# The down projection of a decoder layer as seven block products over sliding ranges of k pairs

## The reference

```python
def _conv_ffn(xn, s_ffn, p):
    u = xn @ p['ffn_w_in']                          # 2048 -> 2 * 5632
    u, buf = _causal_dwconv(u, s_ffn, ...)
    a, b = jnp.split(u, 2, axis=-1)
    return (jax.nn.silu(a) * b) @ p['ffn_w_out'], buf   # 5632 -> 2048
...
    f, f_new = _conv_ffn(xn, s_ffn, p)
    x = x + _rmsnorm(f, p['n_ffn_post'])
```

## Time and profile before

| | |
|---|---|
| time, median of 3 runs | 2547.48 us (2547.18 to 2551.67) |
| time of the profiled execution | 2549.71 us |
| its span, first to last instruction | 2547.8 us |
| PE busy | 2497.7 us, 98% |
| DVE busy | 1620.7 us, 64% |
| ACT busy | 921.5 us, 36% |
| POOL busy | 392.0 us, 15% |
| moved by transfers | 303.32 MB |

### The profile page before, as it was taken

The page is one execution under the profiler, slowest core; times in us unless marked ns, Lnnn a source line. Parts: engine busy times, 40 slices in busy tenths (PEclk is TensorE's granted clock), DMA queues, the critical chain, the costliest instruction groups (busy, mean ns, idle before and its releaser), DMA issues. The chain is left out here.

```text
span 2547.8 us, 48784 instructions
## 1 busy us (share of the span) xinstructions
PE 2497.7 (98%) x20582; PEld 2467.6 (97%) x20582; DVE 1620.7 (64%) x2395; ACT 921.5 (36%) x1324; POOL 392.0 (15%) x208
## 2 busy tenths in 40 slices
PE   7999999999999999999999999999999999999997
PEld 7999999999999999999999999999999999999996
DVE  6544545766146368898889888888998333333226
ACT  5332222433214235444444444444445212122112
POOL 3333222433233352000000000000000000000005
PEclk9999999999999999999999999999999999999998
DMA  4222237622373424233333333333335423232422
GB/s 174 90 82 93 76 111 263 216 76 73 108 257 111 157 67 143 93 98 112 108 114 109 106 106 110 109 106 114 114 106 170 150 75 130 91 122 95 157 84 88
DMA packets 97415, 303.32 MB, mean 119 GB/s; under 512 B 10160, under 2 KB 14896, under 8 KB 96320
## 3 DMA queue, kind: packets, MB, share of 16 engines
q1 hardware_dynamic: 58336, 211.84, 26.3%
q10 hardware_dynamic: 38880, 88.59, 9.6%
HBM read 255.77 MB, written 44.62 MB: 118 GB/s over the span
## 5 line engine op out<-in xcount | busy, mean ns | idle before, releaser
L1313 PE MATMUL psum_proj<-x_hi,w_hi 128*128 128x288 f32 (+2 forms) x1696 | 511.0, 301 | 15.7 <-DVE x_lo L1959 13.6
L1313 PE MATMUL psum_proj<-x_lo,w_hi 128*128 128x288 f32 (+2 forms) x1696 | 501.3, 296 | 0.0
L1315 PE MATMUL psum_proj<-x_hi,w_lo 128*128 128x288 f32 (+2 forms) x1696 | 500.9, 295 | 0.0
L525 POOL TENSOR_TENSOR w_lo<-raw,w_hi 128x1024 fp32r<-128x1024 f32 x128 | 322.0, 2518 | 620.1 <-ACT w_hi L611 620.1
L1313 PEld LDWEIGHTS psum_proj<-x_hi,w_hi 128*128 128x128 f32 x1696 | 320.9, 189 | 23.0 <-issue 16.2
L1313 PEld LDWEIGHTS psum_proj<-x_lo,w_hi 128*128 128x128 f32 x1696 | 320.1, 189 | 2.7 <-issue 1.9
L611 ACT ACTIVATE w_hi<-raw 128x1024 fp32r<-128x1024 f32 x138 | 145.2, 1056 | 487.8 <-PE psum_proj L1315 412.3
L1315 PEld LDWEIGHTS psum_proj<-x_hi,w_lo 128*128 128x128 f32 x1696 | 319.9, 189 | 0.0
L1814 PE MATMUL psum_proj<-ops_a,w_hi 128*128 128x288 f32 x890 | 262.3, 295 | 1.1 <-DVE w_lo L2676 0.7
L1816 PE MATMUL psum_proj<-ops_a,w_lo 128*128 128x288 f32 x890 | 262.1, 295 | 0.0
L1815 PE MATMUL psum_proj<-ops_a,w_hi 128*128 128x288 f32 x890 | 261.9, 294 | 0.0
(11 more groups left out here) (428 smaller groups left out, 6255.5 us busy)
## 6 DMA issues: line engine op xcount, KB each, us to landing
raw<-in_weights_dram SPq DMA_DIRECT2D x386, 512.0 KB, 3.6
g_spill<-x_flat ACTq DMA_DIRECT2D x44, 288.0 KB, 2.1
spill<-tail ACTq DMA_DIRECT2D x24, 288.0 KB, 2.1
arena<-in_xT_dram SPq DMA_DIRECT2D x4, 1152.0 KB, 11.3
y_spill<-arena ACTq DMA_DIRECT2D x4, 1152.0 KB, 5.1
h_spill<-arena ACTq DMA_DIRECT2D x8, 576.0 KB, 2.9
x_hi<-h_spill ACTq DMA_DIRECT2D x1, 4608.0 KB, 19.0
x_flat<-g_spill ACTq DMA_DIRECT2D x5, 864.0 KB, 9.0
```

The source lines that it names most:

```text
L525: nc.gpsimd.tensor_tensor(w_lo[:, slot], raw[:, r], w_hi[:, slot].bitcast(F32), ALU.subtract).then_inc(lo_ready, 1)
L1313: nc.tensor.matmul(banks[:, n, 0:b - a], w_hi[:, slot, k], (hi, lo)[part][:, a:b], start=first and part == 0, stop=False)
L1315: mm = nc.tensor.matmul(banks[:, n, 0:b - a], w_lo[:, slot, k], hi[:, a:b], start=False, stop=last)
```

## The change

The down projection is done as the up projection is: seven block products for two output tiles by two k tiles (a k pair, `kp`). The first 42 k tiles make 21 pairs (`DOWN_KP`), the 16 output tiles make 8 pairs j. A step is one (j, kp), 7 * 3 = 21 matmuls; two steps are a unit, and the 84 down units go on in the same loops, rings and routines as the 160 up units (`ALL_UNITS`). The last two k tiles stay as `last_down`.

The seven products are linear in k, so they are summed over k before they are combined. `WINDOWS` cuts the 21 pairs for each j into five ranges of 2 to 5 pairs, shifted against each other from j to j, so that 40 passes (`PASSES`) are run, 8 for each range r. A pass leaves seven products in seven banks, and the next starts one bank further on. `take_pass` on ACT copies them out: in range 0 into the arena, where each j has seven accumulators (`m_of`), later into a staging buffer `m_stage`. From there GpSimd adds them to the accumulators with two accumulating transfers per pass, of four and of three products (590 and 442 thousand bytes), 60 transfers in all for the 30 passes `STAGED`. ACT waits for the previous one (`m_acc`) before it writes its half of `m_stage` again. The last two passes (`BY_VE`) are added by DVE. `combine` on DVE turns the seven accumulators into the output pair.

The gate rows of a pair are read by SP (`kp_load`, 590 thousand bytes), in the same queue as the weights, into one of five slots. DVE makes three sums (`g_first`, `g_second`, `g_third`), ACT the high parts of all seven operands (`g_highs`, 2016 columns) and DVE the low parts (`g_lows`, 2016). `freed` gives the unit after which a slot is free and `g_made_at` the unit at which a pair is made. The input rows of the residual, 16 by 576, come back in two transfers (`h_load`, 10 rows and 6) in SP's queue instead of one in ACT's. The matmuls of the down projection fall from 4224 to 168 * 21 + 192 = 3720.

```diff
+DOWN_KP, DOWN_PAIRS = FT // 2 - 1, KT // 2
+WINDOWS = ((2, 5, 5, 5, 4),) * 4 + ((3, 5, 5, 5, 3),) * 2 + ((4, 5, 5, 4, 3), (5, 5, 5, 3, 3))
+PASSES = [(r, j, sum(WINDOWS[j][:r]), sum(WINDOWS[j][:r + 1])) for r in range(5) for j in range(DOWN_PAIRS)]
+STEPS = [(p, kp) for p, (r, j, first, stop) in enumerate(PASSES) for kp in range(first, stop)]
+FIRST_STEP = [sum(q < p for q, kp in STEPS) for p in range(len(PASSES))]
+END_STEP = [sum(q <= p for q, kp in STEPS) - 1 for p in range(len(PASSES))]
...
+G_SLOTS = 5
...
+BY_VE = (len(PASSES) - 2, len(PASSES) - 1)
+STAGED = [p for p, (r, j, first, stop) in enumerate(PASSES) if r and p not in BY_VE]
...
+DOWN_PRODUCTS = ((A11, G11), (A12, G21), (S2, G2), (S3, G3), (S1, G1), (S4, G22), (A22, G4))
+M_AT = (0, 2, 3, 1, 5, 6, 4)
+M_SPLIT = 4
...
+        def freed(kp):
+            if kp < 4:
+                return WUNITS - 4 + kp // 2
+            if kp == 4:
+                return WUNITS + 2
+            return WUNITS + LAST_USE[kp - G_SLOTS] // 2
+        g_made_at = {WUNITS - 2: 0, WUNITS - 1: 1, WUNITS + 2: 2, WUNITS + 5: 3, WUNITS + 7: 4}
+        for _kp in range(5, DOWN_KP):
+            g_made_at[max(freed(_kp) + 2, max(g_made_at) + 1)] = _kp
...
+            def kp_load(kp):
+                if kp == 4:
+                    sp.wait_ge(taken, DOWN_TAKEN0)
...
+                    sp.wait_ge(g_st, 16 * FT)
+                else:
+                    sp.wait_ge(units_done, W_UNIT0 + freed(kp) + 1)
+                    sp.wait_ge(g_st, 16 * (2 * kp + 2))
+                sp.dma_start(g_sums(kp)[:, 0:1152].rearrange("p (n t) -> p n t", n=2),
+                             g_spill[2 * kp:2 * kp + 2].rearrange("n p t -> p n t")).then_inc(block_in[kp % G_SLOTS], 16)
...
+            for w in range(2, ALL_UNITS + 2):
+                unit = W_UNIT0 + w
                 sp.wait_ge(lo_ready, unit - 1)
-                sp.wait_ge(ws_ready, unit - 1 - W_UNIT0)
+                sp.wait_ge(ws_ready, w - 1)
                 sp.dma_start(raw[:, unit % 2], weights[unit]).then_inc(raw_in[unit % 2], 16)
-            weights_in((DOWN_UNIT0 + 2) // 2, UNITS // 2)
+                for kp in range(DOWN_KP):
+                    if freed(kp) + 3 == w:
+                        kp_load(kp)
...
+                if w == H_FREED + 3:
+                    sp.wait_ge(units_done, W_UNIT0 + H_FREED + 1)
+                    h_load(0, H_FIRST)
...
+            for p in STAGED:
+                j = PASSES[p][1]
+                for half, (first, stop) in enumerate(((0, M_SPLIT), (M_SPLIT, 7))):
+                    pool.wait_ge(*product_out(p, stop - 1))
+                    pool.dma_start(m_of(j, first, stop), m_stage[:, first * HALF:stop * HALF], accum_op=ALU.add)\
+                        .then_inc(m_acc[half], 16)
...
+            def g_highs(kp):
+                act.wait_ge(op_sum, KP + kp + 1)
+                nc.scalar.activation(g_high_part(kp), g_sums(kp), ACT.Copy).then_inc(op_high, 1)
...
+            def take_pass(p):
+                r, j, first, stop = PASSES[p]
+                for q in range(7):
+                    act.wait_ge(*product_done(p, q))
+                    if r == 0:
+                        to = m_of(j, M_AT[q], M_AT[q] + 1)
+                    else:
+                        to = m_stage[:, M_AT[q] * HALF:(M_AT[q] + 1) * HALF]
+                        before = STAGED.index(p)
+                        if before and q in (0, M_SPLIT):
+                            act.wait_ge(m_acc[q // M_SPLIT], 16 * before)
+                    nc.scalar.activation(to, bank(7 * p + q), ACT.Copy).then_inc(part_out, 1)
...
+            for w in range(3, ALL_UNITS):
                 g, u = STD + w // UP_UNITS, w % UP_UNITS
-                more = w + 2 < WUNITS
+                more = w + 2 < ALL_UNITS
+                conv = STD < g <= FT
+                step = 2 * (w - WUNITS)
                 if more:
                     hi_a(w + 2)
...
-                if w == WUNITS - 3:
...
+                if u == 3 and w < WUNITS:
                     p1_copy(g)
+                if step in END_STEP and END_STEP.index(step) not in BY_VE:
+                    take_pass(END_STEP.index(step))
                 if more:
                     hi_s(w + 2)
...
-                if w == WUNITS - 2:
...
-                if w == WUNITS - 2:
...
+                if step + 1 in END_STEP and END_STEP.index(step + 1) not in BY_VE:
+                    take_pass(END_STEP.index(step + 1))
+                if w in g_made_at:
+                    g_highs(g_made_at[w])
...
+            def down_step(s):
+                p, kp = STEPS[s]
+                w, kk = WUNITS + s // 2, s % 2
+                hi, lo = w_slot(w, 0), w_slot(w, 1)
+                first, last = s == FIRST_STEP[p], s == END_STEP[p]
+                if kk == 0:
+                    pe.wait_ge(lo_ready, W_UNIT0 + w + 1)
+                    pe.wait_ge(wl_ready, w + 1)
+                pe.wait_ge(op_low, G_OPS0 + kp + 1)
+                for q, (wp, go) in enumerate(DOWN_PRODUCTS):
+                    if first:
+                        if q == 0:
+                            pe.wait_ge(*(product_out(p - 2, 6) if p >= 2 else (taken, up_taken(FT - 1) + 6 * p)))
+                        elif p >= 1:
+                            pe.wait_ge(*product_out(p - 1, q - 1))
+                        else:
+                            pe.wait_ge(*((part_out, FT - STD) if q == 1 else (taken, up_taken(FT - 1) + q - 1)))
+                    mm = three(bank(7 * p + q), hi[:, 2 * wp + kk], lo[:, 2 * wp + kk], cut(g_high_part(kp), go),
+                               cut(g_low_part(kp), go), first, last)
+                    if last and (q < 6 or kk == 0):
+                        mm.then_inc(tile_mm, 1)
+                if kk:
+                    mm.then_inc(units_done, 1)
...
+            def g_first(kp):
+                f = g_sums(kp).rearrange("p (n t) -> p n t", n=7)
+                ve.wait_ge(*kp_landed(kp % G_SLOTS, kp // G_SLOTS + 1))
+                own(tt_op(f[:, G3:G1 + 1], f[:, G4:G4 + 1].broadcast_to([P, 2, HALF]), f[:, G22:G11 + 1], ALU.subtract))
+                return steps[0]
+            def g_second(kp, first_step):
+                f = g_views(kp)
+                ve.wait_ge(own_step, first_step)
+                own(tt_op(f[G2], f[G1], f[G22], ALU.subtract))
+                return steps[0]
+            def g_third(kp, second_step):
+                f = g_views(kp)
+                ve.wait_ge(own_step, second_step)
+                tt_op(f[G4], f[G21], f[G2], ALU.add).then_inc(op_sum, 1)
+            def g_lows(kp):
+                ve.wait_ge(op_high, G_OPS0 + kp + 1)
+                ve.wait_ge(op_sum, KP + kp + 1)
+                tt_op(g_low_part(kp), g_sums(kp), g_high_part(kp).bitcast(F32), ALU.subtract).then_inc(op_low, 1)
...
+            def take_pass(p):
+                j = PASSES[p][1]
+                for half in range(2):
+                    ve.wait_ge(m_acc[half], accumulated(p))
+                for q in range(7):
+                    ve.wait_ge(*product_done(p, q))
+                    m = m_of(j, M_AT[q], M_AT[q] + 1)
+                    tt_op(m, bank(7 * p + q), m, ALU.add).then_inc(taken, 1)
...
+            for w in range(3, ALL_UNITS):
                 g, u = STD + w // UP_UNITS, w % UP_UNITS
-                if w + 1 < WUNITS:
+                conv, kp = STD < g <= FT, g_made_at.get(w)
+                step = 2 * (w - WUNITS)
+                if w + 1 < ALL_UNITS:
                     direct_lows(w + 1)
-                if w + 2 < WUNITS:
+                if w + 2 < ALL_UNITS:
                     first_step = sums_first(w + 2)
-                if w + 1 < WUNITS:
+                if step in END_STEP and END_STEP.index(step) in BY_VE:
+                    take_pass(END_STEP.index(step))
+                if w + 1 < ALL_UNITS:
                     sum_lows(w + 1)
-                if w + 2 < WUNITS:
+                if kp is not None:
+                    g_first_step = g_first(kp)
+                if w + 2 < ALL_UNITS:
                     second_step = sums_second(w + 2, first_step)
-                if g > STD and u < 2:
+                if kp is not None:
+                    g_second_step = g_second(kp, g_first_step)
+                if conv and u < 2:
                     tap_one(g - 1, u)
-                if w + 2 < WUNITS:
+                if w + 2 < ALL_UNITS:
                     sums_third(w + 2, second_step)
-                if g > STD and u < 2:
+                if kp is not None:
+                    g_third(kp, g_second_step)
+                if conv and u < 2:
                     tap_two(g - 1, u)
...
-                if w == WUNITS - 2:
...
+                if u == 3 and w < WUNITS:
                     evacuate(g)
-            taps_of(FT - 1, 0)
...
+                if w in combined_at:
+                    combine(combined_at[w])
+                if kp is not None:
+                    g_lows(kp)
...
```

(23 more changed lines are left out.)

365 lines of the change are left out of this document (155 added, 210 removed).

## The result

| | before | after |
|---|---|---|
| time, median of 4 runs each | 2549.16 us | 2567.99 us (2566.59 to 2570.01) |
| span of the profiled execution | 2547.8 us | 2564.9 us |
| matmuls and other TensorE instructions | 20582 | 20078 |

The ratio is 1.0074, with a 95% interval from 1.0057 to 1.0091: the changed kernel is slower, although it does 504 matmuls less. The forecast was 2557 us, 11 less than measured.

The account below looks back on a forecast made before the run. TensorE, busy 2497.7 of 2547.8 us, was taken to bound the kernel. 2549.7 - 66.7 (matmuls) - 0.7 (old waits) + 74.3 (new waits) + 2 (clock) = 2558.6 us profiled; the median, 2.2 lower, 2557 us; range 2510 to 2605.

Parts of the forecast that it names:

- the case that the prediction gave as its forecast: Whole kernel: new TensorE waits of 68 to 85 us, time 2550 to 2567 us; chance 0.38.
- rival 2: Down projection: accumulations fill the transfer engines, weights come late, ScalarE waits for m_acc; 2585 to 2620 us; 0.17 with all above 2567.
- The gain: Down projection on TensorE: 504 fewer matmuls at 0.1323 us each save 66.7 us, also the break-even for new waits.
- What makes the waits: Down projection: preparing a pair takes 5.5 us or more of VectorE's queue against 2.2 us room, delaying the next weights.
- Rival 1: Down projection: VectorE, 77% busy, hides nearly all; up to 35 us of waits, 2480 to 2515 us; 0.22 for below 2534.
- waits for L1225: Sign in the down stage: TensorE would have few waits for ScalarE's copies if the forecast was right.
- The waits by stretch: Last up group to tail tiles: queues moved forward give 74.3 us at factor 2, 17.8 of it in units 63 to 83.
- The accumulations: Accumulating transfers cost twice their bytes in engine time, 5.3 us per interval; waits sum to 74.3 us, against 62.7 at factor 1.
- the 6 that the prediction named as a sign of it: Accumulating transfers landing after 6 us or more, with VectorE waiting for raw all along, would point to rival 2.
- The transfers in front of weights: SP's queue: weights land 1.5 us later behind one pair load, 3.0 behind two; a 2.95 MB h_load adds 7.6 us.
- The clock: TensorE starts matmuls slowly after long waits, which also lets VectorE catch up: 2 us added, between 0 and 6.
- 2.2 us between profiled execution and median: Last step of the sum: the median of runs taken 2.2 us below the profiled execution, 2558.6 us becoming 2557.

Follow-up runs that it names:

- fewer_mm: Kernel before the change with 504 of the 4032 matmuls of down_tile left out, nothing else: 2484.38 us beside 2550.43 (ratio 0.9750).
- lows_late: Changed kernel with g_lows of pairs 2 to 20 moved on VectorE behind the low parts of the next unit's weights: 2542.81 us beside 2550.43 (ratio 0.9965).
- all three reorderings: Changed kernel with lows_late, first residual load cut into five, and second load of pairs freed together issued one unit later: 2535.63 us beside 2550.95.
- acc_small: Changed kernel with each of the 60 accumulating transfers moving 32 columns in place of 1152 or 864: 2555.07 us beside 2550.43 (ratio 1.0026).
- warm_fill: Changed kernel with 27 matmuls without use before the waits for pairs 6, 11 and 16: 2566.01 us beside 2548.49 (ratio 1.0068).

## Why the prediction was right

The direction and the path were right; of the size, half was. The forecast was 9.5 us more than the 2547.48 of the kernel before, and measured are 18.8 more than 2549.16. 2568.0 lies 1 us above the case that the prediction gave as its forecast (2550 to 2567), in the band that it had left to rival 2 and all above, and the runs show that rival 2 is not what happened. (The 2557 is 2556.4 by its own terms.) The terms one by one:

- **The gain**, 504 by 0.1323 = 66.7 us: 66.0 by `fewer_mm`.
- **What makes the waits**: in the main as predicted. TensorE waits for low parts of weights and of pairs in clusters, VectorE's idle time before `g_lows` is put down to L1205 (59.6 us in 20 waits), and moving the one instruction gives back 26 us. Rival 1 (VectorE is 77% busy, so all is hidden) fell for the reason given against it: what counts is not VectorE's share but how long the weights stand behind a pair. Not as predicted: waits for L1225 are not few (9.0 us in 8). For 12 of the 28 waits, 28 us and half of the idle time, the trace names no releaser ("issue"); that the pairs cause them is argued from the order on VectorE, but for what `lows_late` took away, and after all three reorderings 50.6 us are left, 14 of which are about what the accumulations cost.
- **The waits by stretch**: 74.3 us predicted, 82.8 measured, and each stretch within 1.2 us but units 63 to 83, which have 22.0 in place of 17.8. The queues moved by hand leave out the clock, and the measured values have it in them, so part of this nearness is luck.
- **The accumulations**: factor 2 taken, 2.2 measured; 11.7 us of the sum, 14 measured. ScalarE did not wait for `m_acc` before its copies but once, 0.4 us, so rival 2 did not come about, although the transfers of three products landed after 7.2 us, more than the 6 that the prediction named as a sign of it. The Trainium skill, Collectives: The Full Stack, section "The bandwidth ceiling: the fold count and why AG ≠ RS ≠ AR", says that an add needs two source reads; the factor of 2.2 agrees. The fit of the Trainium skill, DMA: Bandwidth & Descriptors, section "Anatomy of one DMA — SWDGE (gpsimd) path" (2.0 us + bytes / 436 GB/s), gives as an estimate 3.4 us for four products and 3.0 for three. The plain copies took 3.3 and 4.0 us, so that the first agrees and the second does not; the additions took 5.2 and 7.2.
- **The transfers in front of weights**: with both kinds of load reordered 4 and 6 us less, neither clear of the noise. The large load (2.95 MB, the first of `h_load`; the prediction calls it the second) was taken as 7.6 us in front of weights that need 3.6 themselves, 11.2 together; these weights landed after 18.8, and after 12.2 in `acc_small`. So it was mis-sized where the accumulations run beside it, in the one stretch that is far off.
- **The clock**, "I add 2 us, between 0 and 6." The slow starts take 22.4 us. In return the idle time is 60.4 us (55.9 and the 28 times 0.16) where the queues alone gave 74. The two together are 8.5 us more than the 74.3; of these, 2.3 are the accumulations by their measured cost, so that about 6 are left for the clock and for every error of the queues moved by hand together. No run separates them: `warm_fill` took 6.2 us of slow starts away for 2.2 us of span. I had in mind only waits as long as the 3.92 us one. In the trace about 15 slow starts follow a wait of 1.50 and one of 1.96 us as well.
- The rest of the 11 us: the forecast took 2.2 us between profiled execution and median away; after, the median is 1.3 above its profiled execution (2566.7). That is 3.5 us of it and says nothing of the kernel.

What stays open: how far filled matmuls help by the clock; how the 26 us of `lows_late` divide between the standing and the work; what VectorE's 70.7 us of waits for weights cost TensorE; and what the waits for ScalarE's copies (L1225) would be worth with another order on ScalarE, which was not tried.

## What to carry to other kernels

Where one engine prepares two streams for another, look at how far ahead it works and at what it stands for in its queue, not at its busy share: here VectorE had 30% free and still made TensorE wait, and a move of one instruction behind the urgent ones was worth 1%. Fewer matmuls are worth their full time only if the waits that the new work brings, and the slow matmuls behind them, are smaller; advance the queues by the durations of the trace before writing such a change. An accumulating transfer from SBUF to SBUF is to be counted at about twice its bytes.

## What the runs showed of the hardware

- An accumulating transfer from SBUF to SBUF took 2.2 times the engine time of the plain copy of the same bytes (6.7% against 3.1% of 16 engines' span), and 5.2 us to landing against 3.3 for 590 thousand bytes.
- A subtraction on VectorE beside one on GpSimd, all operands in SBUF, does not share: 3.13 us in place of 0.95, until 0.82 us after GpSimd's end.
- Slow starts of matmuls (0.24 us apart, at a granted clock of 0.50, which is 1.2 GHz) followed some waits of 1.5 to 2 us. The length of the wait alone does not decide it: one of 3.10 us in front of unit 50 was followed by none in one execution and by 16 in another.
- 524 thousand bytes of weights, issued half a microsecond behind 2.95 MB in the same queue, landed after 18.8 us, where 3.6 is the median.
